# A key search's closing mask from tie count and stored signs, with the first heads' norm factors made by ScalarE and GpSimd

## The chip, the cores and the metric

The kernel runs on one core of a Trainium2 chip, as one launch. The metric is the device time in microseconds (us), as the median of several executions. TensorE does the matrix products, VectorE, ScalarE and GpSimd work on tiles of 128 partitions, and SyncE starts the transfers. In rows of the profile they are PE (PEld for its weight loads), DVE, ACT, POOL and SP.

## The reference

The program is a streaming encoder of two layers over 1024 positions of width 1024. The first layer is a sparse attention: an indexer gives each query a score for every admissible key, the 256 best keys are kept, and a grouped-query attention (16 heads in 4 groups, head size 64) runs over them, with RMS-normalised queries and keys. A banded attention and two convolutional feed-forward blocks follow.

```python
def dsa_mixer(h, w_in, q_g, k_g, t5_table):
    proj = h @ w_in
    q, k, v, qi, ki, wi = jnp.split(proj, list(A_SPLITS), axis=-1)
    q = rmsnorm(q.reshape(B, S, KV_GROUPS, Q_PER_KV, HEAD_DIM), q_g)
    k = rmsnorm(k.reshape(B, S, KV_GROUPS, HEAD_DIM), k_g)
...
        score = jnp.where(admissible[None], score, -jnp.inf)
        sel_score, sel = lax.top_k(score, topk)
        valid = jnp.isfinite(sel_score)
        k_sel = jax.vmap(lambda kb, ib: kb[ib])(k, sel)
```

`rmsnorm` divides by the root of the mean square of the 64 numbers of a head, plus 1e-6. On ties `top_k` keeps the keys that come first.

## The kernel before

The program is a chain of stages, each a block with one hand-written order of instructions per engine. An engine waits only on semaphores within a block, and all engines meet between two blocks. The head stage makes the scores SC, a tile with 4224 columns: six query tiles of 128 rows (tiles 2 to 7) that see 384, 512, 640, 768, 896 and 1024 keys, one behind the other. The first two query tiles see at most 256 keys and need no search.

The search stage (`select_phase`) finds for each query the value TH between kept and dropped keys. VectorE first turns the scores into ordered integers (ORD), then does two times 16 rounds, one bit each, over the high and then the low half of these integers. In a round VectorE counts the keys below TH in three of the six spans and ScalarE, by the sum of signs, in the other three. Three operations on 128x6 numbers close a round on VectorE: INC (was the count small enough), TH (the new threshold) and LESS (the half step of the next round). In the same stage TensorE makes the projections of queries, keys and values: four weight groups of eight tiles, 24 matmuls of 128x384 each. The weights come in two buffers, one transfer per group; the third group's transfer starts when TensorE has done its eighth tile. Each group is split into a high part WH (a cast) and a low part WL (a difference) in two halves; TensorE waits for the low parts (`w_lo`). For the first group ScalarE makes the casts and for the others GpSimd does. ScalarE takes the projected tiles out of PSUM (`take`), one per round, and the last three behind its signs.

At the end of the search VectorE marks the keys equal to TH and counts them (EQ, CNT, six operations), ranks these ties with six scans (RANK), and ScalarE sums the signs of TH minus the keys (SGN) into a scrap tile. From CNT and SGN follows how many ties may stay (ROOM). Six DROP operations mark the ties of too high a rank, and six MASK operations join them with the keys below TH.

The attention stage (`dsa_phase`) works in passes over pairs of heads. In the first pass it also makes the first group's queries and keys: GpSimd squares a tile's five heads (`raw_square`), VectorE sums them (`variance`), GpSimd takes the power -0.5 (`root`) and multiplies into DUP (`scaled`), TensorE turns DUP into TQ, ScalarE and VectorE split it into high and low part, and the logits follow. GpSimd's order is square 0, square 1, root 0, DUP 0, the blanking of the bias tile BB, and then square, root and DUP of one tile after the other. The other three groups are made the same way during later passes.

## Time and profile before

| what | value |
|---|---|
| median of 3 runs | 3011.78 us (3011.35 to 3015.06) |
| profiled execution | 3010.81 us |
| its span, first to last instruction | 3008.6 us |
| granted TensorE clock, mean | 0.973 |
| TensorE matmuls | busy 2792.0 us (93%) |
| VectorE | 1525.4 us (51%) |
| ScalarE | 1111.2 us (37%) |
| GpSimd | 840.1 us (28%) |
| mean of GpSimd's 128x1024 low part (L291, 132 times) | 2523 ns |

The busy times overlap, so they say which engine has the most work and not which one sets the end of a stage. A granted clock of 1.0 is TensorE's full 2.4 GHz, 0.5 is 1.2 GHz. For a change that touches the seam of two stages, the instructions in order of time around the seam are the rows to read.

### The profile page before, as it was taken

How to read it: one execution, taken by the hardware profiler on the slowest of the kernel's cores; microseconds unless marked ns; L12 is line 12 of the kernel's file. 1: busy time of each engine (PE TensorE's matmuls, PEld its weight loads, DVE VectorE, ACT ScalarE, POOL GpSimd, SP SyncE). 2: the span in 40 equal slices, each digit the busy share in tenths (PEclk: the TensorE clock that was granted, in tenths of full speed). 3: DMA queues.
4: the chain of work that ended last, by engine and by line, in shares of the span. 5: the costliest groups of instructions: out<-in, count | busy, mean ns of one | idle time of the engine just before them, and what ended most of it. 6: DMA issues, size and time to landing. Idle time of an engine off the chain costs nothing. (4 is left out here: it accounts for less than half of the span.)

```text
span 3008.6 us, 38734 instructions
## 1 busy us (share of the span) xinstructions
PE 2792.0 (93%) x14678; PEld 2388.8 (79%) x14678; DVE 1525.4 (51%) x2431; ACT 1111.2 (37%) x2392; POOL 840.1 (28%) x479
## 2 busy tenths in 40 slices
PE   6797698999999999999989986888999999999999
PEld 5697587887788888888879986777877888888887
DVE  5899665651544444544441113777515444444444
ACT  4677465551322222222245534666413222222221
POOL 4021523202332232232244431111023223232221
PEclk9899799999999999999989998999999999999999
DMA  4110000011211111111031100001012111111111
GB/s 162 42 43 1 25 5 8 14 52 42 71 49 49 42 43 54 42 50 50 12 130 43 43 21 1 12 26 68 8 36 77 50 42 52 45 42 56 49 42 63
DMA packets 38754, 132.43 MB, mean 44 GB/s; under 512 B 4240, under 2 KB 12608, under 8 KB 36960
## 3 DMA queue, kind: packets, MB, share of 16 engines
q1 hardware_dynamic: 38624, 130.68, 13.0%
q8 instruction: 83, 1.36, 0.2%
q14 instruction: 47, 0.39, 0.0%
HBM read 122.22 MB, written 13.69 MB: 45 GB/s over the span
## 5 line engine op out<-in xcount | busy, mean ns | idle before, releaser
L330 PE MATMUL banks<-XH,WH 128*128 128x512 f32 x1408 | 446.1, 397 | 5.3 <-POOL WL L291 4.2
L330 PE MATMUL banks<-XL,WH 128*128 128x512 f32 x1408 | 444.2, 396 | 0.0
L330 PE MATMUL banks<-XH,WL 128*128 128x512 f32 x1408 | 444.1, 396 | 0.0
L291 POOL TENSOR_TENSOR WL<-WR,WH 128x1024 fp32r<-128x1024 f32 x132 | 332.1, 2523 | 389.4 <-ACT WH L245 389.4
L260 ACT ACTIVATE Y<-U,CONVB,CONVW 128x1024 f32<-128x1024 f32 x88 | 109.5, 1244 | 659.7 <-DVE U L386 659.7
L386 DVE TENSOR_TENSOR U<-banks,RB 128x1024 f32<-128x1024 f32 x88 | 107.8, 1225 | 433.8 <-PE banks L330 424.5
L330 PEld LDWEIGHTS banks<-XH,WH 128*128 128x128 f32 x1408 | 265.4, 189 | 70.4 <-POOL WL L291 4.4
L330 PEld LDWEIGHTS banks<-XL,WH 128*128 128x128 f32 x1408 | 265.6, 189 | 64.2
L330 PEld LDWEIGHTS banks<-XH,WL 128*128 128x128 f32 x1408 | 265.3, 188 | 64.2
L376 DVE TENSOR_TENSOR XT<-XT,banks 128x1024 f32<-128x1024 f32 x176 | 214.6, 1219 | 164.7 <-PE banks L346 164.7
L299 POOL TENSOR_TENSOR AL<-Y,AH 128x1024 fp32r<-128x1024 f32 x44 | 106.0, 2410 | 625.5 <-ACT AH L268 625.5
L346 PE MATMUL banks<-AH,WH 128*128 128x512 f32 x704 | 219.4, 393 | 0.2 <-DVE XT L376 0.2
L346 PE MATMUL banks<-AL,WH 128*128 128x512 f32 x704 | 217.0, 389 | 0.0
L346 PE MATMUL banks<-AH,WL 128*128 128x512 f32 x704 | 216.8, 389 | 0.0
L245 ACT ACTIVATE WH<-WR 128x1024 fp32r<-128x1024 f32 x132 | 136.2, 1046 | 195.8 <-PE banks L346 101.7
L394 DVE SCALAR_TENSOR_TENSOR Y<-U,CONVW,Y 128x1022 f32<-128x1022 f32 x88 | 197.5, 2244 | 8.8 <-DVE Y L388 0.9
L771 PE MATMUL banks<-QWH,XH 128*128 128x384 f32 x512 | 179.1, 350 | 8.5 <-POOL QWL L717 8.5
L388 DVE SCALAR_TENSOR_TENSOR Y<-U,CONVW,Y 128x1023 f32<-128x1023 f32 x88 | 113.0, 1284 | 138.1 <-ACT Y L260 138.1
L771 PE MATMUL banks<-QWL,XH 128*128 128x384 f32 x512 | 177.6, 347 | 0.0
L771 PE MATMUL banks<-QWH,XL 128*128 128x384 f32 x512 | 176.7, 345 | 0.0
L346 PEld LDWEIGHTS banks<-AH,WH 128*128 128x128 f32 x704 | 130.6, 188 | 32.4 <-DVE XT L376 6.1
L346 PEld LDWEIGHTS banks<-AL,WH 128*128 128x128 f32 x704 | 132.2, 188 | 28.0
(225 smaller groups left out, 5462.9 us busy)
## 6 DMA issues: line engine op xcount, KB each, us to landing
WR<-in_ffn SPq DMA_DIRECT2D x132, 512.0 KB, 3.4
QWR<-in_qkv SPq DMA_DIRECT2D x12, 1536.0 KB, 6.7
XT<-in_xT SPq DMA_DIRECT2D x16, 512.0 KB, 7.8
OWR<-in_w_o SPq DMA_DIRECT2D x16, 512.0 KB, 3.2
spill<-XT SPq DMA_DIRECT2D x8, 512.0 KB, 14.6
XT<-spill SPq DMA_DIRECT2D x8, 512.0 KB, 7.1
outT<-XT SPq DMA_DIRECT2D x8, 512.0 KB, 2.6
near<-strip SPq DMA_DIRECT2D x1, 3072.0 KB, 21.3
```

Of the source, the lines that this page charges most:

```text
L245: act.activation(WH[:, ch % RING, :], WR[:, ch % RING, :], ACT.Copy).then_inc(w_hi, 1)
L260: act.activation(Y[:, j, k, :], U[:, k, :], ACT.Identity, bias=c.CONVB[:, layer, bass.ds(tap, 1)], scale=c.CONVW[:, layer, 2, bass.ds(tap, ...
L291: pool.tensor_tensor(WL[:, ch % RING, :], WR[:, ch % RING, :], WH[:, ch % RING, :].bitcast(F32), ALU.subtract).then_inc(w_lo, 1)
L299: pool.tensor_tensor(AL[:, g % 2, j, :], Y[:, j, 0, :], AH[:, g % 2, j, :].bitcast(F32), ALU.subtract).then_inc(a_lo, 1)
L330: mm = pe.matmul(u[:, h * HALF:(h + 1) * HALF], w[:, ch % RING, db * P:(db + 1) * P], x[:, db, h * HALF:(h + 1) * HALF], start=(db == 0 an ...
L346: mm = pe.matmul(DN[db % 2][:, h * HALF:(h + 1) * HALF], w[:, (ch + j) % RING, db * P:(db + 1) * P], x[:, g % 2, j, h * HALF:(h + 1) * HAL ...
L376: dve.tensor_tensor(c.XT[:, db, :], c.XT[:, db, :], DN[db % 2][:], ALU.add).then_inc(dn_free, 1)
L386: dve.tensor_tensor(U[:, k, :], UP[k][:], RB[:], ALU.mult).then_inc(scaled, 1)
L388: dve.scalar_tensor_tensor(Y[:, j, k, 1:S], U[:, k, 0:S - 1], c.CONVW[:, layer, 1, bass.ds(tap, 1)], Y[:, j, k, 1:S], ALU.mult, ALU.add).t ...
L394: dve.scalar_tensor_tensor(Y[:, j, k, 2:S], U[:, k, 0:S - 2], c.CONVW[:, layer, 0, bass.ds(tap, 1)], Y[:, j, k, 2:S], ALU.mult, ALU.add).t ...
L771: mm = pe.matmul(PJ[t % len(PJ)][:, 0:PROJ], x[:, db, i * P:(i + 1) * P], w[k % 2][:, db, :], start=(db == 0 and x is c.XH and w is WH), s ...
```

## The change

The signs of ScalarE are stored: SIDE holds, for each key, the sign of key minus TH (-1, 0 or 1), with the negated threshold NTH as bias. One operation per span then makes the mask: (RANK > ROOM) > SIDE is true for every key below TH (the left side is 0 or 1, and both are above -1), for a tie of too high a rank (1 > 0), and never for a key above TH. DROP and its six operations are gone, and so are ScalarE's waits between its signs. NTH is one operation more on VectorE, before the tie counts.

The mean squares of the first group's eight tiles are made in the search stage: after its last takes ScalarE runs 40 squares (8 tiles by 5 heads), each with its sum, and GpSimd makes variance and power -0.5 of all 40 numbers at once, into ROOTS. In the attention stage the first group's squares, variances and roots are gone, GpSimd starts with DUP 0 and DUP 1, and BB is blanked behind them. The casts of the first weight group move from ScalarE to GpSimd.

```diff
@@ -1163,24 +1164,26 @@
 
             def raw_square(t):
                 raw = c.qkv(t)[:, 0:NH * HD]
-                if t >= 2:
-                    pool.wait_ge(summed, t - 1)
+                if t >= TT + 2:
+                    pool.wait_ge(summed, t - TT - 1)
                 pool.tensor_tensor(SQ[:, t % 2, :], raw, raw, ALU.mult).then_inc(squared, 1)
 
             def root(t):
-                pool.wait_ge(var_ready, t + 1)
+                pool.wait_ge(var_ready, t - TT + 1)
                 pool.tensor_tensor(RS[:, t % TT, 0:NH], VAR[:, t % 2, 0:NH], c.NHALF[:, 0:NH],
                                    ALU.pow).then_inc(rs_ready, 1)
 
             def scaled(t):
-                pool.wait_ge(rs_ready, t + 1)
+                root_of = ROOTS[:, t, :] if t < TT else RS[:, t % TT, 0:NH]
+                if t >= TT:
+                    pool.wait_ge(rs_ready, t - TT + 1)
                 if t >= 2:
                     pool.wait_ge(turned, round_of_tile(t - 2) + 1)
                 pool.tensor_tensor(
                     DUP[:, t % 2, :].rearrange("p (h k d) -> p h k d", h=NH, k=2),
                     c.qkv(t)[:, 0:NH * HD].rearrange("p (h d) -> p h d", h=NH).unsqueeze(2)
                     .to_broadcast([P, NH, 2, HD]),
-                    RS[:, t % TT, 0:NH].unsqueeze(2).unsqueeze(3).to_broadcast([P, NH, 2, HD]),
+                    root_of.unsqueeze(2).unsqueeze(3).to_broadcast([P, NH, 2, HD]),
                     ALU.mult).then_inc(dup_ready, 1)
 
             def output_weights(db):
...
@@ -1188,15 +1191,11 @@
                 pool.tensor_tensor(OL[:, db % 2, :], OR[:, db % 2, :], OH[:, db % 2, :].bitcast(F32),
                                    ALU.subtract).then_inc(o_lo, 1)
 
-            raw_square(0)
-            raw_square(1)
-            for t in range(TT):
-                root(t)
+            scaled(0)
+            scaled(1)
+            pool.memset(BB[:, :, :, 0:S - W], 0.0).then_inc(b_blank, 1)
+            for t in range(2, TT):
                 scaled(t)
-                if t == 0:
-                    pool.memset(BB[:, :, :, 0:S - W], 0.0).then_inc(b_blank, 1)
-                if t + 2 < TT:
-                    raw_square(t + 2)
             for k in range(1, GROUPS):
                 for i in range(TT + 1):
                     if i < TT:
...
@@ -1320,12 +1319,12 @@
         @block.vector
         def _(dve):
             def variance(t):
-                dve.wait_ge(squared, t + 1)
-                if t >= 2:
-                    dve.wait_ge(rs_ready, t - 1)
+                dve.wait_ge(squared, t - TT + 1)
+                if t >= TT + 2:
+                    dve.wait_ge(rs_ready, t - TT - 1)
                 dve.tensor_reduce(SSQ[:, t % 2, 0:NH], SQ[:, t % 2, :].rearrange("p (h d) -> p h d", h=NH), AX.X,
                                   ALU.add).then_inc(summed, 1)
-                dve.wait_ge(summed, t + 1)
+                dve.wait_ge(summed, t - TT + 1)
                 dve.tensor_scalar(VAR[:, t % 2, 0:NH], SSQ[:, t % 2, 0:NH], 1.0 / HD, EPS, ALU.mult,
                                   ALU.add).then_inc(var_ready, 1)
 
...
@@ -1376,18 +1375,14 @@
                                   OP[:, 0:PAIR].rearrange("p (h d) -> p h d", h=2),
                                   RCP[:].unsqueeze(2).to_broadcast([P, 2, HD]), ALU.mult).then_inc(mo_ready, 1)
 
-            variance(0)
-            variance(1)
             queries_low(0, 0)
             others_low(0, None, 1)
-            variance(2)
             dve.wait_ge(b_blank, 1)
             mask(0)
             row_max(0)
             row_max(1)
             queries_low(1, 2)
             others_low(1, None, 3)
-            variance(3)
             row_max(2)
             queries_low(2, 4)
             others_low(2, None, 5)
...
@@ -1397,8 +1392,6 @@
                 if i >= 4:
                     dve.wait_ge(t_first, g + 1)
                     dve.tensor_copy(PT[:, g % 2, 0:HALF], TP[0][:]).then_inc(pt_dve, 1)
-                if p == 0 and h == 0 and i + EARLY + 1 < TT:
-                    variance(i + EARLY + 1)
                 if g + AHEAD < ALL:
                     row_max(g + AHEAD)
                 if has_round(g):
...
@@ -1848,13 +1841,16 @@
     with ExitStack() as ctx:
         sem, old = c.signals.open(ctx, f"s")
         QT = TT - FIRST_TOP
+        NH = DSA.nh
         m = Map(nc, c.after_scores, c.before_qkv)
         MASK, SC = c.MASK, c.SC
         ORD = nc.alloc_sbuf_tensor_at("ORD", [P, SC_ALL], I32, offset=c.scores_at)
         RANK = nc.alloc_sbuf_tensor_at("RANK", [P, SC_ALL], F32, offset=c.scores_at)
         REST = m.take("REST", [P, SC_ALL], F32)
         LOW = nc.alloc_sbuf_tensor_at("LOW", [P, SC_ALL], U16, offset=m.at)
-        DROP = m.take("DROP", [P, SC_ALL], BF16)
+        SIDE = m.take("SIDE", [P, SC_ALL], BF16)
+        SSQ = m.take("SSQ0", [P, TT, NH], F32)
+        VAR = m.take("QVAR0", [P, TT, NH], F32)
         EQ = MASK
         JUNKA = m.take("JUNKA", [P, 3, S], BF16)
         WH = m.take("QWH", [P, 2, DB, PROJ], F32R)
...
@@ -1906,12 +1904,15 @@
             pool.sem_clear(old)
             for k in range(GROUPS):
                 for h in range(2):
-                    if k >= 1:
-                        pool.wait_ge(w_landed[k % 2], 16 * (k // 2 + 1))
-                        pool.tensor_copy(WH[:, k % 2, half(h), :], WR[:, k % 2, half(h), :]).then_inc(w_hi, 1)
+                    pool.wait_ge(w_landed[k % 2], 16 * (k // 2 + 1))
+                    pool.tensor_copy(WH[:, k % 2, half(h), :], WR[:, k % 2, half(h), :]).then_inc(w_hi, 1)
                     pool.wait_ge(w_hi, 2 * k + h + 1)
                     pool.tensor_tensor(WL[:, k % 2, half(h), :], WR[:, k % 2, half(h), :],
                                        WH[:, k % 2, half(h), :].bitcast(F32), ALU.subtract).then_inc(w_lo, 1)
+            pool.wait_ge(squared, TT)
+            pool.tensor_scalar(VAR[:], SSQ[:], 1.0 / HD, EPS, ALU.mult, ALU.add).then_inc(var_ready, 1)
+            pool.wait_ge(var_ready, 1)
+            pool.tensor_tensor(c.ROOTS[:], VAR[:].rearrange("p t h -> p (t h)"), c.NHALF[:], ALU.pow)
 
         @block.tensor
         def _(pe):
...
@@ -1946,9 +1947,6 @@
                     if src is LOW and BETWEEN.stop + j < TILES - 3:
                         take(BETWEEN.stop + j)
 
-            act.wait_ge(w_landed[0], 16)
-            for h in range(2):
-                act.activation(WH[:, 0, half(h), :], WR[:, 0, half(h), :], ACT.Copy).then_inc(w_hi, 1)
             act.wait_ge(done, 2)
             count_signs(halves[:, :, 1], HIGH_STEP)
             act.wait_ge(done, K_REST + 1)
...
@@ -1958,13 +1956,19 @@
             for t in BETWEEN:
                 take(t)
             count_signs(LOW, LOW_STEP)
-            act.wait_ge(stepped, LOW_STEP + BITS)
+            act.wait_ge(done, K_END + 1)
             for q, off, n in spans:
-                act.activation(JUNKA[:, 0, 0:n], REST[:, off:off + n], ACT.Sign, bias=TH[:, q:q + 1], scale=-1.0,
+                act.activation(SIDE[:, off:off + n], REST[:, off:off + n], ACT.Sign, bias=NTH[:, q:q + 1],
                                accum_out=SGN[:, q:q + 1]).then_inc(signed, 1)
-                act.wait_ge(signed, spans.index((q, off, n)) + 1)
             for t in range(TILES - 3, TILES):
                 take(t)
+            junk = JUNKA[:].rearrange("p a n -> p (a n)")
+            for t in range(TT):
+                for h in range(NH):
+                    mm = act.activation(junk[:, (t * NH + h) * HD:(t * NH + h + 1) * HD],
+                                        c.qkv(t)[:, h * HD:(h + 1) * HD], ACT.Square,
+                                        accum_out=SSQ[:, t, h:h + 1])
+                mm.then_inc(squared, 1)
 
         @block.vector
         def _(dve):
...
@@ -2006,27 +2010,24 @@
             dve.wait_ge(done, K_END)
             find(LOW, LOW_STEP, BITS)
             dve.wait_ge(stepped, LOW_STEP + BITS)
+            dve.tensor_scalar(NTH[:], TH[:], -1.0, None, ALU.mult).then_inc(done, 1)
             for q, off, n in spans:
                 dve.tensor_scalar(EQ[:, off:off + n], REST[:, off:off + n], TH[:, q:q + 1], None, ALU.is_equal,
                                   ALU.add, accum_out=CNT[:, q:q + 1]).then_inc(done, 1)
             for q, off, n in spans:
                 eq = EQ[:, off:off + n]
-                dve.wait_ge(done, K_END + q + 1)
+                dve.wait_ge(done, K_END + q + 2)
                 dve.tensor_tensor_scan(RANK[:, off:off + n], eq, eq, 0.0, ALU.add, ALU.max).then_inc(done, 1)
 
-            k = K_END + 2 * QT
+            k = K_END + 1 + 2 * QT
             dve.wait_ge(signed, QT)
-            dve.tensor_tensor(INC[:], CNT[:], SGN[:], ALU.add).then_inc(done, 1)
+            dve.tensor_tensor(INC[:], CNT[:], SGN[:], ALU.subtract).then_inc(done, 1)
             dve.wait_ge(done, k + 1)
             dve.scalar_tensor_tensor(ROOM[:], INC[:], 0.5, CONST[:], ALU.mult, ALU.add).then_inc(done, 1)
             dve.wait_ge(done, k + 2)
             for q, off, n in spans:
-                dve.scalar_tensor_tensor(DROP[:, off:off + n], RANK[:, off:off + n], ROOM[:, q:q + 1],
-                                         EQ[:, off:off + n], ALU.is_gt, ALU.mult).then_inc(done, 1)
-            for q, off, n in spans:
-                dve.wait_ge(done, k + 3 + q)
-                dve.scalar_tensor_tensor(MASK[:, off:off + n], REST[:, off:off + n], TH[:, q:q + 1],
-                                         DROP[:, off:off + n], ALU.is_lt, ALU.add).then_inc(done, 1)
+                dve.scalar_tensor_tensor(MASK[:, off:off + n], RANK[:, off:off + n], ROOM[:, q:q + 1],
+                                         SIDE[:, off:off + n], ALU.is_gt, ALU.is_gt).then_inc(done, 1)
 
 
 class Chip:
...
@@ -2053,7 +2054,8 @@
         c.MH, c.ML = c.XH, c.XL
         c.IDF = m.take("IDF", [P, P], F32)
         c.ONES = m.take("ONES", [P, P], F32)
-        c.NHALF = m.take("NHALF", [P, TT], F32)
+        c.NHALF = m.take("NHALF", [P, TT * DSA.nh], F32)
+        c.ROOTS = m.take("ROOTS", [P, TT * DSA.nh], F32)
         c.RSTD = m.take("RSTD", [P, TT], F32)
         c.GAIN = m.take("GAIN", [P, 4, DB], F32)
         c.HGAIN = m.take("HGAIN", [P, 4], F32)
...
```

Not shown are declarations: new tiles for NTH, the name ROOTS in the attention stage, and the two semaphores `squared` and `var_ready` in the search stage.

## Rows read from the trace of the kernel before

**Rows 1.** Stretch, its length, busy us of PE, PEld, DVE, ACT, POOL; clock, DMA, GB/s.

```profile
284.30:310.10 25.80, 0.58 (x4) 0.26 (x2) 25.06 (x32) 7.37 (x15) 0.00 (x0) 0.59 0.00 0
```

**Rows 2.** VectorE in order of time (start us, us, engine, line, operation).

```profile
284.32 0.75 DVE L2010 TENSOR_SCALAR_CACHE_REDUCE MASK<-REST,TH 128x512 bf16<-128x512 f32 x1
...
299.01 5.26 DVE L2024 SCALAR_TENSOR_TENSOR DROP<-RANK,ROOM,MASK 128x512 bf16<-128x512 f32 x6
...
304.19 5.26 DVE L2028 SCALAR_TENSOR_TENSOR MASK<-REST,TH,DROP 128x512 bf16<-128x512 f32 x6
```

**Rows 3.** GpSimd in order of time, opening of the attention stage.

```profile
310.11 1.40 POOL L1168 TENSOR_TENSOR SQ<-QKVA 128x320 f32<-128x320 f32 x2 [76.37 <-POOLq L1848]
...
312.88 1.26 POOL L1179 TENSOR_TENSOR DUP<-QKVA,RS 128x640 f32<-128x640 f32 x1
314.08 2.66 POOL L1197 MEMSET BB<- 128x3072 f32 x1
```

**Rows 4.** ScalarE in order of time, end of the search.

```profile
281.54 0.82 ACT L1942 ACTIVATE JUNKA<-LOW,TH 128x640 bf16<-128x640 uint16 x1
...
282.36 1.13 ACT L1942 ACTIVATE JUNKA<-LOW,TH 128x1024 bf16<-128x1024 uint16 x1
...
290.36 1.52 ACT L1935 ACTIVATE QKVB<-banks,RSTD 128x384 f32<-128x384 f32 x3
```

**Rows 5.** ScalarE in order of time, the later stage's squares.

```profile
1562.45 0.31 ACT L641 ACTIVATE JUNK<-banks,RSTD 128x64 bf16<-128x64 f32 x1
...
1562.74 0.31 ACT L641 ACTIVATE JUNK<-banks,RSTD 128x64 bf16<-128x64 f32 x1
```

**Rows 6.** GpSimd's roots, one line of each place (ns min/median/max).

```profile
L1172 POOL TENSOR_TENSOR RS<-QVAR,NHALF x32: 1167/1167/1169, 311.6 to 550.4; 128x5 f32<-128x5 f32 x32
...
L1658 POOL TENSOR_TENSOR RSTD<-VAR,NHALF x1: 1652/1652/1652, 47.7 to 47.7; 128x8 f32<-128x8 f32 x1
...
L157 POOL TENSOR_TENSOR RSTD<-VAR,NHALF x3: 2619/2619/2621, 775.4 to 2266.2; 128x8 f32<-128x8 f32 x3
```

**Rows 7.** ScalarE in order of time, start of the search.

```profile
142.02 2.86 ACT L1951 ACTIVATE QWH<-QWR 128x1536 fp32r<-128x1536 f32 x2 [8.73 <-DMA QWR<-in_qkv]
```

**Rows 8.** GpSimd in order of time, weights of the projections.

```profile
143.58 6.88 POOL L1913 TENSOR_TENSOR QWL<-QWR,QWH 128x1536 fp32r<-128x1536 f32 x2 [75.19 <-ACT QWH L1951]
150.40 1.46 POOL L1911 CAST QWH<-QWR 128x1536 fp32r<-128x1536 f32 x1
151.94 3.50 POOL L1913 TENSOR_TENSOR QWL<-QWR,QWH 128x1536 fp32r<-128x1536 f32 x1
...
190.20 1.47 POOL L1911 CAST QWH<-QWR 128x1536 fp32r<-128x1536 f32 x1 [29.75 <-DMA QWR<-in_qkv]
```

**Rows 9.** TensorE in order of time, projections and the attention's second turn.

```profile
147.07 0.69 PE L1926 MATMUL banks<-QWH,XH 128*128 128x384 f32 x1 [15.12 <-POOL QWL L1913]
...
152.04 0.49 PE L1926 MATMUL banks<-QWH,XH 128*128 128x384 f32 x1
...
284.55 0.34 PE L1926 MATMUL banks<-QWH,XL 128*128 128x384 f32 x1
...
319.93 1.11 PE L1224 MATMUL banks<-IDF,DUP 128*128 128x128 f32 x4 [0.61 <-POOL DUP L1179]
```

**Rows 10.** VectorE in order of time, in the search.

```profile
138.20 4.56 DVE L1989 TENSOR_TENSOR ORD<-SC,REST 128x4224 int32<-128x4224 int32 x1
...
147.52 2.95 DVE L1980 TENSOR_TENSOR INC<-CNT,KEEP 128x6 f32<-128x6 f32 x1 [1.53 <-ACT JUNKA L1942]
...
151.91 3.56 DVE L1974 TENSOR_SCALAR LESS<-TH,BITF 128x6 f32<-128x6 f32 x1
...
158.16 2.31 DVE L1980 TENSOR_TENSOR INC<-CNT,KEEP 128x6 f32<-128x6 f32 x1
...
190.77 0.92 DVE L1980 TENSOR_TENSOR INC<-CNT,KEEP 128x6 f32<-128x6 f32 x1
```

**Rows 11.** GpSimd in order of time, first feed-forward stage.

```profile
778.03 7.66 POOL L291 TENSOR_TENSOR WL<-WR,WH 128x1024 fp32r<-128x1024 f32 x2
```

More of the change, by code:

```diff
@@ L1016, in dsa_phase @@
         RS = m.take("RS0", [P, TT, 8], F32)
+        ROOTS = c.ROOTS[:].rearrange("p (t h) -> p t h", h=NH)
         NM = m.take("NM0", [P, 8], F32)
@@ L1865, in select_phase @@
         LESS = m.take("LESS", [P, QT], F32)
+        NTH = m.take("NTH", [P, QT], F32)
         INC = m.take("INC", [P, QT], F32)
@@ L1874, in select_phase @@
         counted, off_done, signed = sem("counted"), sem("off_done"), sem("signed")
+        squared, var_ready = sem("squared"), sem("var_ready")
         w_landed = [sem("w_even"), sem("w_odd")]
```

## The prediction

> **What bounds the kernel now.** I read the page first. TensorE is busy for 93% of the span (the table above), but that is a mean over stages, and the change sits in the one long hole: the table of stretches shows TensorE with 0.58 us of work in the 25.8 us from 284.3 to 310.1, VectorE with 25.06 and the granted clock down at 0.59 [rows 1]. There the engines' order of time decides, so I read the timeline of each engine. VectorE works without a gap: tie marks and counts from 284.32, six scans, six DROP operations (5.26), six MASK operations (5.26), ended at 309.45 [rows 2]. Then the next stage opens: GpSimd's first instruction at 310.11, 0.66 us after VectorE's end, and two squares, a root and the first DUP follow; the DUP, which TensorE waits for, starts at 312.88 [rows 3]. So the path is: end of the search, VectorE to 309.45, 0.66 of stage change, 2.77 of GpSimd work, DUP. ScalarE has nothing to do after about 291.9 [rows 4]. That free time is what the change fills, and the question is whether the filling ends before VectorE does.
>
> **VectorE's part.** DROP goes: minus 5.26. The new MASK operation has DROP's operands (an f32 tile, a column, a bf16 tile), so it costs 5.26, as DROP did. One small NTH operation comes in: LESS, its like, has its successor 0.14 us after it, so plus 0.14. VectorE would end at 304.3 (309.45 - 5.26 + 0.14).
>
> **ScalarE's part.** The signs start after NTH, at 284.31 + 0.22 = 284.53 (0.17 to run and 0.05 to signal; an estimate). Without the waits between them they run as the search's own counts do: 640 elements take 0.82 from start to start; for 1024 the sum starts 1.04 and the next operation would start 1.13 after the start (as long as the record is) [rows 4]. That is 0.30 + 0.81 per 1000 elements, and six signs over 4224 elements give 1.8 + 3.4 = 5.2: ended at 289.7. The three takes need 1.5 [rows 4]: 291.2. Then forty squares of 64 elements, each with a sum. The nearest row is the later stage's squares, one per 0.29 us from start to start, reading PSUM [rows 5]: 11.6 us. By the line just fitted for SBUF sources, 64 elements take 0.30 + 0.05 = 0.35: 14.0. The new squares read SBUF, so I take nearly that, 0.335 (13.4). The squares end at 304.6; the bounds are 302.8 and 305.2.
>
> **GpSimd's part.** The variance of 40 elements has no row; the bounds are 0.1 (nothing but a signal) and 0.8, and I take 0.3 plus 0.2 of signals. The root is a power of 128x40. Rows: 1.167 us for 5 elements, 1.652 for 8, and another stage's 2.62 for 8 [rows 6]. The first two give 0.162 per element and 0.36 fixed; 40 elements are then 6.8 us. With 2.62 the slope is 0.282 and the root 11.6. The 5-element roots work on the very numbers that the new root works on and never differ by more than 2 ns, so I take 6.8. GpSimd ends at 304.6 + 0.5 + 6.8 = 311.9, later than VectorE's 304.3 and later than the old end, 309.45. The stage change, again 0.66, leads to 312.6, where DUP is now the first instruction: before it was 312.88. The 5.26 taken from VectorE and the 2.77 taken from the opening come to 8.0, and the new chain on ScalarE and GpSimd gives back 7.7: **minus 0.3** (from -2.8 with the cheap squares and variance to +5.6 with dear squares, variance and root).
>
> **The opening of the attention.** The second DUP no longer waits for a root: TensorE's 0.61 of idle time ahead of its turn at 319.93 goes [rows 9], and the turns behind it, each of which waits for the one before, pass that on. The eight variances leave VectorE too, at a place where it mostly waits for the others; I give them 0.1 of gain. The blanking of BB (2.66) now stands behind two DUPs of 1.26 [rows 3], from 2.5 to 5.2 us after the first DUP's start. Its reader needs the first logits as well, and these stand just ahead of TensorE's turn at 319.93, some 6 us after that start [rows 3, 9], so the blanking costs nothing; with a faster first turn it would cost what it sticks out. Sum: **minus 0.7** (0 to -1.7).
>
> **The other end: the first weight group.** ScalarE made the high part of group 0 in 2.86 us from 142.02 [rows 7]; now GpSimd does, in front of each of its two low parts. GpSimd's pace is 4.99 us per half: 1.54 from a cast's start to its low part's, and 3.45 for the low part (two took 6.88) [rows 8]. These are the dangerous rows, because VectorE's smallest operations stand still behind GpSimd's: INC, normally 0.17, took 2.95 and ended with GpSimd's low part at 150.5; LESS took 3.56, just as long as the low part from 151.94 [rows 8, 10]. The counts themselves run beside it: from that LESS's end at 155.45 to the next INC at 158.16 they take 2.7, with a cast and a low part running [rows 10]. The reverse happens too: two of GpSimd's operations of a kind that takes 2.5 on average (the table above) took 7.66 beside VectorE's [rows 11]. So GpSimd's first cast, whose weights are there at 142.02, should wait for VectorE's ORD, which ends at 142.76 [rows 10].
>
> The Trainium skill (SBUF — State Buffer, "SBUF: two separate sides") calls the pair of ports that the two engines share an exclusive lock, held for the whole instruction, also by a VectorE operation with two SBUF inputs when GpSimd reads SBUF. By it the cast starts at 142.8; without it at 142.0, and the sum of this part would be 0.5 instead of 1.3. The trace agrees with the rule at every small operation named above.
>
> Step by step, with halves at 142.80, 147.79, 152.78 and 157.77, GpSimd is done at 162.8 (before 160.45). LESS waits for the cast (144.3), counts to 147.0, INC waits to 147.8, TH to 149.3, LESS to 152.8, counts to 155.5, INC to 157.8, TH to 159.3, LESS to 162.8, counts to 165.5, TH done 166.0. Before, the INC of 158.16 ended at 160.5 and its TH 0.3 later, and the third TH, one undisturbed round of 3.4 on, at 164.1 [rows 10]: the search is 1.9 late here. TensorE: its first low part is ready at 147.75 (0.7 late); twelve matmuls at 0.33 (147.07 to 152.04 are fifteen steps) [rows 9] bring it to 151.7, and the second low part comes at 152.75, a wait of 1.1. Before, sixteen had started by 152.04, and the rest went at 0.176 (752 in 132.5 us) [rows 9]. Its thirteenth now starts at 152.8, six or seven full-speed steps behind, and a first matmul is 0.17 longer: 1.3 late. If the pause keeps the clock at 0.5 for some ten matmuls more, add 1.5: 2.8.
>
> Group 2's weights start after TensorE's eighth tile, so GpSimd's conversion of 190.20 [rows 8] moves by TensorE's 1.3, to 191.5, and its cast ends at 193.0. INC, issued at 190.77 [rows 10], comes 1.9 later, at 192.6, still inside the cast. So it is released in the same place as before, TH and LESS too, and the search leaves group 2 late by exactly GpSimd's shift, 1.3; group 3 keeps the same distance. TensorE's own 1.3 are covered: ScalarE takes the last tiles at 290.36, 5.5 us after the last matmul began [rows 4, 9]. **Plus 1.3** for the rest of the kernel (0.5 to 2.8; 4.0 with the rival below).
>
> **Sum.** -0.3 - 0.7 + 1.3 = +0.3 us. The profiled execution took 3010.81 for a span of 3008.6 (2.2 lie around it) and is 1.0 under the median of 3011.78. So 3011.1 for a like execution, 3012.1 as a median. This kernel's measurement can tell 0.2% (6 us) from no change.
>
> **Rivals.** (1) *VectorE sets the end*, since squares and root are cheaper than their rows: DUP starts at 304.3 + 0.66 = 305.0 instead of 312.88; -7.9 - 0.7 + 1.3 = -7.3, 3004.5. For it speaks only the change's arithmetic; against it the 0.29 per square even at the lower bound, which puts ScalarE's end at 302.8 and leaves 1.5 us for variance and root. Chance 0.05. (2) *The root is dear*, on the other side: GpSimd's 40-element power at 0.282 per element costs 11.6, +4.8: +5.1, 3016.9. It is slower by over 0.2% from 0.31 per element on. The other stage's row speaks for it, the 32 equal 5-element rows against. Chance 0.11. (3) *The search loses a slot*: if TensorE is under 1.0 late, or the search over 2.2, INC at group 2 meets the 3.5 us low part instead of the cast; counts that had run beside the second low part then run behind it, +2.7: +3.0, 3014.8. My margin is 0.35 us. Chance 0.15. (4) *The moved cast costs nothing in the search* and the squares go by the lower bound: -0.3 - 1.8 - 0.7 = -2.8, 3009.0. Chance 0.10. The forecast itself: 0.59, with its own range of 3010 to 3014.
>
> **How the numbers follow.** The range takes in (3) and (4) and most of (2): 3008.5 to 3017. Faster by over 0.2% needs (1): 0.06, with a little for what I do not see. Slower by over 0.2% needs (2) with (3) or with the dear bounds of other terms: 0.09. Within 0.2%: 0.85.
>
> **What would show it.** The last MASK operation near 305.6 (304.3 + 1.3), the squares ending near 305.9, the 128x40 power lasting 6.8 and ending near 313, the first DUP 0.7 us after it, at 313.9 against 312.88. In the search: the first INC ending at 147.8, the third TH at 166.0, the group 2 cast at 191.5, the first tie count at 285.8 instead of 284.32. Wrong would be a power far from 6.8, squares far from 0.335 apart, or a search end that is not TensorE's shift.

## The result, and the profile after

The changed kernel takes **2988.0 us** (2985.2 to 2991.5) against 3013.4 (3011.4 to 3015.6) for the kernel before on the same chip: ratio 0.9916, with an interval of 0.9899 to 0.9933. It is 25 us faster, where 3012.1 was forecast and 3008.5 was the bottom of the range. The profiled execution has a span of 2985.7 (before 3008.6), and the mean granted clock is 0.972 against 0.973, so the clock is not the answer.

First the place where the change was made. The kernel after, VectorE, ScalarE, GpSimd and TensorE at the end of the search, in order of time on each engine (start us, us, engine, line, operation):

```profile
303.01 5.28 DVE L2029 SCALAR_TENSOR_TENSOR MASK<-RANK,ROOM,SIDE 128x512 bf16<-128x512 f32 x6
...
293.65 1.49 ACT L1936 ACTIVATE QKVB<-banks,RSTD 128x384 f32<-128x384 f32 x3
295.04 0.25 ACT L1968 ACTIVATE JUNKA<-QKVA 128x64 bf16<-128x64 f32 x1
...
295.28 0.25 ACT L1968 ACTIVATE JUNKA<-QKVA 128x64 bf16<-128x64 f32 x1
...
304.77 1.07 POOL L1913 TENSOR_SCALAR QVAR<-SSQ 128x40 f32<-128x40 f32 x1 [67.12 <-ACT JUNKA L1968]
305.93 6.98 POOL L1915 TENSOR_TENSOR ROOTS<-QVAR,NHALF 128x40 f32<-128x40 f32 x1
313.57 2.47 POOL L1182 TENSOR_TENSOR DUP<-QKVA,ROOTS 128x640 f32<-128x640 f32 x2 [0.67 <-POOLq L1841]
...
314.88 1.11 PE L1223 MATMUL banks<-IDF,DUP 128*128 128x128 f32 x4 [27.74 <-POOL DUP L1182]
```

The first DUP starts at 313.57; before it started at 312.88 [rows 3], and 313.9 was forecast. So the seam is 0.7 us later than before, and nothing was won there. The first matmul of each stage says where the 22.9 us of span went. TensorE's rows of the kernel before, in order of time:

```profile
314.19 1.12 PE L1224 MATMUL banks<-IDF,DUP 128*128 128x128 f32 x4 [29.31 <-POOL DUP L1179]
...
672.72 0.48 PE L1285 MATMUL banks<-XH,OWH 128*128 128x512 f32 x1
...
1529.37 0.69 PE L771 MATMUL banks<-QWH,XH 128*128 128x384 f32 x1 [8.31 <-POOL QWL L717]
...
2163.41 0.48 PE L848 MATMUL banks<-XH,OWH 128*128 128x512 f32 x1
```

and of the kernel after (its first matmul of the attention, 314.88, is shown above):

```profile
674.91 0.48 PE L1284 MATMUL banks<-XH,OWH 128*128 128x512 f32 x1
...
1522.09 0.69 PE L771 MATMUL banks<-QWH,XH 128*128 128x384 f32 x1 [8.71 <-POOL QWL L717]
...
2151.80 0.48 PE L848 MATMUL banks<-XH,OWH 128*128 128x512 f32 x1
```

| stage | before | after | difference |
|---|---|---|---|
| up to the attention's first matmul | 314.19 | 314.88 | +0.7 |
| attention | 358.53 | 360.03 | +1.5 |
| output projection and feed-forward | 856.65 | 847.18 | -9.5 |
| second projections and attention | 634.04 | 629.71 | -4.3 |
| output projection and feed-forward | 845.19 | 833.90 | -11.3 |

All of the gain lies in stages whose code the change doesn't touch, and there it is spread evenly. One place in the second feed-forward, TensorE in order of time, shows it. Before:

```profile
2399.68 0.63 PE L330 MATMUL banks<-XL,WH 128*128 128x512 f32 x2
2400.15 0.63 PE L330 MATMUL banks<-XH,WL 128*128 128x512 f32 x2
2400.62 0.63 PE L330 MATMUL banks<-XH,WH 128*128 128x512 f32 x2
```

After:

```profile
2399.61 0.62 PE L330 MATMUL banks<-XH,WH 128*128 128x512 f32 x2
2400.06 0.62 PE L330 MATMUL banks<-XL,WH 128*128 128x512 f32 x2
2400.52 0.62 PE L330 MATMUL banks<-XH,WL 128*128 128x512 f32 x2
```

There is no bracket with idle time in either; the clock is full. Two matmuls take 0.47 from start to start before and 0.455 after. Over hundreds of steps (572 and 573 between 1000 and 1200 us, those of over 300 ns left out) the pace is **233.3 ns before and 229.0 after** for 128x512 (L330), and 176.0 against 173.3 for 128x384 (L771, over 1,000 each). The down-projections (L346) stay at 227.1 and 227.5. There are 4,224 matmuls of L330, 768 of the two output projections (232.4 to 228.9) and 1,536 of L771: 4,224 x 4.35 ns is 18.4, 768 x 3.5 is 2.7 and 1,536 x 2.67 is 4.1, together 25.2 us, and the last three rows of the table give 25.1. The kernels' instructions are the same there; what differs is the SBUF address of their tiles. The change widened NHALF from 8 to 40 numbers and added ROOTS, another 40, ahead of nearly everything in the memory map: the tiles of these stages lie 320 bytes higher. XH and XL, allocated ahead of NHALF, stay.

### The profile page after: what moved, and what is told of

Its sections match the earlier page's. It is cut to its first block and busy times, and to the rows that moved or that the text cites. A ratio compares the mean times of both kernels' runs of the same rounds, so it can differ in the third digit from the quotient of the medians.

```text
span 2985.7 us, 38732 instructions
## 1 busy us (share of the span) xinstructions
PE 2768.3 (93%) x14646; PEld 2387.3 (80%) x14678; DVE 1518.5 (51%) x2410; ACT 1117.7 (37%) x2470; POOL 837.7 (28%) x467
## 5 line engine op out<-in xcount | busy, mean ns | idle before, releaser
L330 PE MATMUL banks<-XH,WH 128*128 128x512 f32 x1408 | 439.8, 394 | 5.0 <-POOL WL L291 4.2
L330 PE MATMUL banks<-XL,WH 128*128 128x512 f32 x1408 | 440.5, 394 | 0.0
L330 PE MATMUL banks<-XH,WL 128*128 128x512 f32 x1408 | 436.4, 391 | 0.0
L330 PEld LDWEIGHTS banks<-XH,WH 128*128 128x128 f32 x1408 | 265.5, 189 | 62.8 <-POOL WL L291 4.3
L330 PEld LDWEIGHTS banks<-XH,WL 128*128 128x128 f32 x1408 | 265.3, 188 | 61.0
L330 PEld LDWEIGHTS banks<-XL,WH 128*128 128x128 f32 x1408 | 265.6, 189 | 58.0
L346 PE MATMUL banks<-AH,WH 128*128 128x512 f32 x704 | 218.8, 392 | 0.0
L346 PE MATMUL banks<-AL,WH 128*128 128x512 f32 x704 | 217.4, 390 | 0.0
L346 PE MATMUL banks<-AH,WL 128*128 128x512 f32 x704 | 216.8, 389 | 0.0
L771 PE MATMUL banks<-QWH,XH 128*128 128x384 f32 x512 | 177.8, 347 | 8.9 <-POOL QWL L717 8.9
L771 PE MATMUL banks<-QWL,XH 128*128 128x384 f32 x512 | 176.3, 344 | 0.0
L771 PE MATMUL banks<-QWH,XL 128*128 128x384 f32 x512 | 175.4, 343 | 0.0
L346 PEld LDWEIGHTS banks<-AH,WH 128*128 128x128 f32 x704 | 130.6, 188 | 30.6 <-DVE XT L376 4.5
L346 PEld LDWEIGHTS banks<-AH,WL 128*128 128x128 f32 x704 | 132.1, 188 | 28.2
```

What stands on the lines that cost most here:

```text
L330: mm = pe.matmul(u[:, h * HALF:(h + 1) * HALF], w[:, ch % RING, db * P:(db + 1) * P], x[:, db, h * HALF:(h + 1) * HALF], start=(db == 0 an ...
L346: mm = pe.matmul(DN[db % 2][:, h * HALF:(h + 1) * HALF], w[:, (ch + j) % RING, db * P:(db + 1) * P], x[:, g % 2, j, h * HALF:(h + 1) * HAL ...
L771: mm = pe.matmul(PJ[t % len(PJ)][:, 0:PROJ], x[:, db, i * P:(i + 1) * P], w[k % 2][:, db, :], start=(db == 0 and x is c.XH and w is WH), s ...
```

## The experiments

Two theories were open after that. *Placement*: TensorE's pace hangs on the addresses; padding alone gives the gain and the change at the old addresses gives none of it. *The change's own work*: freeing VectorE and GpSimd at the seam speeds something up later. A matmul's row names two operands: the one with 128*128 is called stationary here, the one with 512 or 384 columns moving. Below, "distance" is the address of the moving tile minus that of the stationary one in L330, modulo 256 bytes: XH lies at 33,920 and WH of the feed-forward at 119,040, so it is 128 before and 64 after (XL and WL lie at the same places modulo 256). The expectations of pad320_again and pad192 count it the other way round, so that their 192 is 64 here and their 64 is 192.

**pad320.** The kernel before, with an unused tile of 320 bytes behind NHALF:

```
 c.NHALF = m.take("NHALF", [P, TT], F32)
+m.take("PAD", [P, 80], F32)
```

> The kernel before with one unused tile of 320 bytes per partition behind NHALF, so that every tile behind it lies 320 bytes higher, as in the changed kernel; no instruction changes. Theory A, placement: the pace of the matmuls follows where the stationary and the moving operand lie in SBUF. Then the up-projections (L330) go at 0.229 us from start to start instead of 0.233 and the band projections at 0.173 instead of 0.176, and the kernel takes 2988 to 2991. Theory B, the change's own instructions gave the time: the pace stays at 0.233 and the time at 3013.

Measured: 2994.6 (2993.5 to 2997.6), ratio 0.9931 [0.9918, 0.9945]; L330 at 229.0. Twenty of the 25 us come from a tile that nobody reads; the 2988 to 2991 of the expectation was missed by 4. In this profile L771 ran at 176.7; the very same kernel, profiled once more, is below.

**after_old.** The whole change, with every tile of before at its old address: NHALF 8 wide, the 40-wide constant and ROOTS in a gap behind other tiles, SSQ, VAR and NTH behind the old tiles of the select stage.

```
-c.NHALF = m.take("NHALF", [P, TT * DSA.nh], F32)
-c.ROOTS = m.take("ROOTS", [P, TT * DSA.nh], F32)
+c.NHALF = m.take("NHALF", [P, TT], F32)
+c.XHALF = nc.alloc_sbuf_tensor_at("XHALF", [P, TT * DSA.nh], F32, offset=c.before_qkv - 384)
+c.ROOTS = nc.alloc_sbuf_tensor_at("ROOTS", [P, TT * DSA.nh], F32, offset=c.before_qkv - 192)
```

> The changed kernel with all tiles that the kernel before has at their old addresses (the new tiles ROOTS, SSQ, VAR, NTH and a 40-element exponent tile lie in room that was free). Theory A: the matmul paces are those of before, 0.233 and 0.176, and only the seam is left: 3011 to 3014, within 0.2% of before. Theory B: 2988 as the changed kernel.

Measured: 3012.2 (3006.2 to 3013.9), ratio 0.9989 [0.9980, 0.9998]; L330 at 233.3. This is the edit as the prediction had priced it. GpSimd and TensorE in order of time:

```profile
303.48 6.98 POOL L1916 TENSOR_TENSOR ROOTS<-QVAR,XHALF 128x40 f32<-128x40 f32 x1
311.13 2.47 POOL L1182 TENSOR_TENSOR DUP<-QKVA,ROOTS 128x640 f32<-128x640 f32 x2 [0.67 <-POOLq L1842]
...
312.44 1.12 PE L1223 MATMUL banks<-IDF,DUP 128*128 128x128 f32 x4 [26.04 <-POOL DUP L1182]
```

**The mask alone and the casts alone.** mask_old has only SIDE, NTH and the one mask operation (norm factors and casts as before, old addresses); after_old_casts is after_old with the first group's casts back on ScalarE.

```
(in short)
-ACT.Sign, bias=TH[:, q:q + 1], scale=-1.0        (into JUNKA)
+ACT.Sign, bias=NTH[:, q:q + 1]                   (into SIDE)
-DROP = (RANK > ROOM) * EQ ;  MASK = (REST < TH) + DROP
+MASK = (RANK > ROOM) > SIDE
```

> The kernel before with the first half of the change alone: the signs stored in SIDE and one mask operation per span; norm factors as before, the first weight group's casts on ScalarE, all old tiles at their old addresses. My theory of the seam: VectorE ends 5.1 us earlier, nothing else moves, so the time falls by 5.1 us (ratio 0.9983) and the paces are those of before. Rival: the second half carries part of the gain, and this half alone gives under 3 us.

> The changed kernel with all old tiles at their old addresses and the first weight group's two casts back on ScalarE. My theory: the search loses nothing any more, so it is 1.3 to 1.5 us faster than the same kernel with the casts on GpSimd, and about 4 us faster than before (ratio 0.9986). Rival: the casts cost nothing where they are, and the time is that of the kernel with casts on GpSimd (0.9989).

Measured: mask_old 3009.6 (3005.4 to 3011.7), ratio 0.9983 [0.9974, 0.9992]; after_old_casts 3009.3 (3007.6 to 3011.8), ratio 0.9982 [0.9973, 0.9991]. mask_old, GpSimd and TensorE:

```profile
306.11 1.39 POOL L1168 TENSOR_TENSOR SQ<-QKVA 128x320 f32<-128x320 f32 x2 [71.27 <-POOLq L1848]
...
308.88 1.26 POOL L1179 TENSOR_TENSOR DUP<-QKVA,RS 128x640 f32<-128x640 f32 x1
...
310.19 1.11 PE L1224 MATMUL banks<-IDF,DUP 128*128 128x128 f32 x4 [24.60 <-POOL DUP L1179]
```

The mask alone starts the attention at 310.19, earlier than the whole change (312.44). The early norm factors add 1.6 to it (311.75 in after_old_casts), and the moved casts another 0.7. The three intervals overlap, so the times don't tell these kernels apart, nor whether the casts cost the 1.3 to 1.5 us of the expectation; the order is that of the profiles.

**Which addresses.** More or less padding, and the whole map moved by 128 bytes with XH and XL in it, so that no distance changes:

```
+m.take("PAD", [P, 16], F32)      (pad64; 32, 48, 64 numbers for pad128, pad192, pad256)

-m = Map(nc, (nc.sbuf_base + 63) // 64 * 64, top - 2 * 4 * S)
+m = Map(nc, (nc.sbuf_base + 63) // 64 * 64 + 128, top - 2 * 4 * S)      (base128)
```

> The kernel before with 64 bytes more in front of the later tiles. Theory A with a period of 256 bytes in the distance between the two operands: weights then lie at 64 modulo 256 and XH at 128, as after the change, so L330 goes at 0.229 and the kernel takes about 2990. If the size of the shift matters in another way (period 1024 or more), the pace can stay at 0.233.

> The kernel before with 128 bytes more in front of the later tiles: weights and XH then have the same address modulo 256, as weights and AH of the down-projections have already (0.228). Theory A with a period of 256 in the distance: L330 at 0.228 to 0.229. If what counts is that the weights' address is no multiple of 128, L330 stays at 0.233.

> The kernel before with all of its SBUF map 128 bytes higher, XT, XH and XL too, so that the distances between weights and XH stay as they were and only the absolute addresses change. If the distance of the two operands sets the pace, L330 stays at 0.233 and the projections at 0.176; if the absolute address of one of them does (weights at 128 modulo 256, as with the 128 bytes of padding behind XH), L330 goes at 0.227.

> The kernel before with 256 bytes more in front of the tiles behind NHALF. If the pace repeats every 256 bytes of distance, L330 is back at 0.233 and the time at about 3013; if only the old place was bad, it is 0.227 to 0.229.

> 192 bytes of padding, the last of the four places modulo 256: the weights' distance to XH is then 64 modulo 256. If the pace depends on how far the distance is from 128, L330 goes at 0.229, as with 64 and 320 bytes (distance 192); time about 2994. A pace of 0.227 or 0.233 would say that the dependence is not symmetric.

> The very kernel with 320 bytes of padding once more. Its band projections went at 0.1767, though all tiles of that stage lie where the changed kernel has them, which went at 0.1733. If such a pace changes from execution to execution, it may now read 0.1733; if the program fixes it, 0.1767 again. L330 at 0.229 in either case.

| kernel | distance | L330 | L771 | L346 | out. proj. to end | time |
|---|---|---|---|---|---|---|
| before | 128 | 233.3 | 176.0 | 227.1 | 2335.9 | 3010.8 |
| after_old | 128 | 233.3 | 176.0 | 226.9 | 2333.5 | 3012.2 (median) |
| base128 | 128 | 233.3 | 176.0 | 227.1 | 2335.8 | 3014.5 |
| pad256 | 128 | 233.3 | 176.0 | 227.1 | 2335.7 | 3011.2 |
| pad64 | 64 | 229.0 | 173.3 | 227.4 | 2312.8 | 2996.1 |
| pad320 | 64 | 229.0 | 176.7 | 227.6 | 2317.2 | 2994.6 (median) |
| pad320_again | 64 | 229.0 | 173.3 | 227.3 | 2311.0 | 2994.5 |
| after | 64 | 229.0 | 173.3 | 227.5 | 2310.8 | 2988.0 (median) |
| pad128 | 0 | 226.7 | 173.3 | 227.2 | 2301.9 | 2983.9 |
| pad192 | 192 | 233.3 | 173.3 | 227.1 | 2332.8 | 3011.3 |

(Paces in ns from start to start, steps of over 300 ns left out, L330 and L346 from 1000 to 1200 us and L771 from 1580 to 1760; the last column but one from the first output projection's start to the end of the span; times in us, where not a median, of the profiled execution. In L771 the weights move and XH is stationary, so there 64 and 192 change places.) The pace goes by the distance and not by either address alone: the weights stand 128 bytes higher in pad128 and in base128 alike, and only the one where XH stays is fast. The down-projections move with their own input AH, keep their distance of 0, and their pace, whether both operands stand 0, 64, 128 or 192 bytes behind a multiple of 256: most of their steps are 226 or 227 ns, as in the up-projections of pad128. (The expectation's 0.228 for them has a few pauses of over 300 ns in its mean.) Distances of 64 and 192 were each run with one pair of addresses modulo 256 only. Each of the two extreme cases in the second feed-forward, TensorE in order of time. pad128:

```profile
2399.59 0.62 PE L330 MATMUL banks<-XH,WH 128*128 128x512 f32 x2
2400.04 0.62 PE L330 MATMUL banks<-XL,WH 128*128 128x512 f32 x2
2400.49 0.61 PE L330 MATMUL banks<-XH,WL 128*128 128x512 f32 x2
```

base128:

```profile
2399.81 0.63 PE L330 MATMUL banks<-XH,WL 128*128 128x512 f32 x2
2400.28 0.63 PE L330 MATMUL banks<-XH,WH 128*128 128x512 f32 x2
```

pad192 was the miss: with a distance of 192 I had counted on the pace of 64, as if only how far apart the two are mattered. L330 read 233.3 instead. So it matters which of the two is ahead, or 64 and 192 differ for a reason that these runs don't show. The equal means of 128 and 192 hide different steps: at 128 they alternate between 229 or 230 ns and 237 or 238, the long one between the two matmuls that share a stationary tile, and at 192 nearly all are 233 or 234; at 64 they go round 226, 229 and 232. For 384 columns only distance 128 is slow. The pad320 profile's 176.7 at L771 does not come from the placement alone: the same kernel read 173.3 the second time, so one profile's pace at L771 is weaker evidence than L330's, which followed the distance in all 14 profiles.

The times of single executions hold more than the pace. In the profiles of pad64, pad128 and pad320_again the search loses some 4 us near 225 us (told below), and their attention begins at 318.5 to 319.4, where pad320, base128, pad256 and pad192 read 313.6 to 314.8. That is a part of why pad64 missed its 2990.

**The best placement, timed.** pad128 again, and mask_pad128: the mask half of the change with 128 bytes of padding.

> The kernel before with 128 bytes of padding again, now timed. From the paces of its first look (L330 at 0.2267 for 4224 matmuls, 0.0066 less than before: 28 us; band projections 1536 by 0.0027: 4 us; output projections 768 by 0.0055: 4 us; projections of the search stage are behind the search, and the head stage loses about 1): 35 us less than before, 2979 to 2985. Rival: part of that was one lucky execution, and the timed gain is under 26 us.

> The better version from both findings: the first half of the change alone (signs stored, one mask operation), casts on ScalarE, and 128 bytes of padding. If the two gains add, it is 5 us under the kernel with the padding alone, at 2975 to 2980, and faster than the changed kernel (2988) by 8 us or more. Rival: with TensorE at the faster pace the seam no longer counts, and it is level with the padding alone.

Measured: pad128_timed 2979.6 (2978.2 to 2980.2), ratio 0.9885 [0.9869, 0.9902]; mask_pad128 **2972.9** (2972.5 to 2973.5), ratio 0.9865 [0.9848, 0.9881], the fastest kernel of this study, 15 us under the change as made. The padding's gain came as expected. With the mask the time is 6.7 under the padding alone, where 5 was expected, and below the stated 2975 to 2980; the rival (level with the padding alone) is out.

## Why the prediction was wrong

**The step that failed** is one that the prediction took without saying: "**Plus 1.3** for the rest of the kernel", where the rest was carried over unmoved, matmul for matmul. The prediction went through the diff operation by operation, and passed over two lines of it, the allocation of NHALF and ROOTS, as if memory cost nothing. Their effect was -25 us (from 672.72 and 674.91 on, the last three rows of the table of stages), more than three times the largest gain that any rival allowed for. pad320 gets it without the change, after_old loses it with the change.

The Trainium skill (SBUF — State Buffer, "SBUF: two separate sides") says that TensorE never waits on anyone at SBUF's engine ports. No run here tests it against another engine; what they show is that the distance of TensorE's own two operands moves its pace, from 226.7 to 233.3 ns with the same instructions on every engine.

**The edit itself**, at the old addresses, was forecast at +0.3 us and measured at -0.11% of 3012, or -3 us, with an interval from -0.6 to -6; in the profiles the attention begins 1.75 earlier (312.44 against 314.19). That is below the 0.2% that the measurement can tell, and just at the lower edge of the range (0.9989 x 3011.8 = 3008.5). Term by term:

- *Mask in one operation*: right. The six take 5.28, and 5.26 are gone. mask_old starts the attention 4.0 earlier although its tie count starts later; its ratio makes 5 us of it.
- *Squares*: mis-sized. They came every 0.24 us, not 0.335, under even my lower bound of 0.29 [rows 5]. Those squares read PSUM and are scaled by a column of RSTD (`scale=c.RSTD`), while the new ones read SBUF and have no such scale; which of the two makes the difference was not tested. 40 of them: 9.6 instead of 13.4.
- *Variance*: 1.07 for 128x40 on GpSimd where 0.3 was taken, and 1.16 with the signal.
- *Root*: 6.98, taken as 6.8. The 11.6 of the dear root [rows 6] did not come. Rival (2) is out, and so is (1): ScalarE, GpSimd's variance and root still set the end, 5.3 us behind the last MASK (308.29 against 313.57).
- *The low end of this sum*: -2.8 was an error of adding. 302.8 + 0.1 + 6.8 + 0.66 is 310.4, 2.5 under 312.88.
- *The moved casts*: the mechanism was right in after_old, to within 0.5: the first INC ends at 148.1, the third TH starts at 166.0, the third group's conversion at 192.0, where 147.8, 166.0 and 191.5 were said, and TensorE paused 0.74 ahead of 153.09, with a select stage that began 0.5 late. The tie count came 1.0 late beyond that, so the moved cast was not free, as rival (4) had it. GpSimd's first cast did wait for ORD, which ends at 143.92 in the kernel after: its record is 1.91 long instead of 1.46 and ends at 145.25. In the kernel after, the search was 2.8 late rather than 1.3, as much as the prediction's dear case, but not by its steps. The third group's cast started at 194.53, 3.2 late once the stage's own late start is taken off, and INC met the 3.5 us low part there (196.85, below), as rival (3) had it. The search had done one more round before it than in the kernel before, so it did not lose rival (3)'s whole 2.7.

The kernel after, search, in order of time, GpSimd, then VectorE, then TensorE:

```profile
143.34 1.91 POOL L1908 CAST QWH<-QWR 128x1536 fp32r<-128x1536 f32 x1 [73.58 <-DMA QWR<-in_qkv]
...
194.53 1.47 POOL L1908 CAST QWH<-QWR 128x1536 fp32r<-128x1536 f32 x1 [30.87 <-DMA QWR<-in_qkv]
196.08 3.51 POOL L1910 TENSOR_TENSOR QWL<-QWR,QWH 128x1536 fp32r<-128x1536 f32 x1
...
150.22 3.51 DVE L1978 TENSOR_SCALAR LESS<-TH,BITF 128x6 f32<-128x6 f32 x1
...
156.42 2.25 DVE L1984 TENSOR_TENSOR INC<-CNT,KEEP 128x6 f32<-128x6 f32 x1
...
160.12 3.56 DVE L1978 TENSOR_SCALAR LESS<-TH,BITF 128x6 f32<-128x6 f32 x1
...
196.85 2.76 DVE L1984 TENSOR_TENSOR INC<-CNT,KEEP 128x6 f32<-128x6 f32 x1
...
148.81 0.69 PE L1927 MATMUL banks<-QWH,XH 128*128 128x384 f32 x1 [15.69 <-POOL QWL L1910]
...
153.75 0.69 PE L1927 MATMUL banks<-QWH,XH 128*128 128x384 f32 x1 [0.73 <-POOL QWL L1910]
```

The matmul behind the pause took 0.69 and the clock was still halved: fourteen matmuls, the last of them at 158.07, started some 0.32 us apart, where the prediction's dear case had ten. The granted clock of two stretches of four us says the same (stretch, length, busy us of PE, PEld, DVE, ACT and POOL, clock, DMA share, GB/s). Before:

```profile
152.00:156.00 4.00, 4.00 (x23) 4.00 (x23) 4.00 (x2) 2.57 (x6) 4.00 (x2) 0.95 0.01 2
156.00:160.00 4.00, 4.00 (x25) 4.00 (x24) 3.96 (x7) 0.00 (x0) 3.92 (x2) 1.00 0.01 2
```

After:

```profile
152.00:156.00 4.00, 3.27 (x11) 2.76 (x10) 4.00 (x6) 0.87 (x2) 3.92 (x3) 0.50 0.02 4
156.00:160.00 4.00, 4.00 (x19) 4.00 (x18) 3.93 (x4) 0.00 (x0) 4.00 (x2) 0.71 0.01 2
```

The clock that stayed low and the 1.2 us by which the select stage began late (ORD at 139.36 against 138.20 [rows 10]) put ScalarE's signs 2.6 later than forecast (they wait for NTH and start at 288.45, where 284.53 + 1.3 = 285.8 follows from the prediction; VectorE's tie count starts at 288.32); cheap squares give 3.8 back, variance and root take 0.9: 313.9 + 2.6 - 3.8 + 0.9 = 313.6, and 313.57 was measured. The forecast of the seam was nearly right because two errors cancelled.

**A slot like rival (3)'s** was lost elsewhere too. Two profiles of the kernel with 128 bytes of padding reach the attention's first matmul at 319.35 and at 314.10; 1.1 of the 5.25 is there already as the first projection starts. Near 225 us GpSimd converts the last weight group. GpSimd and VectorE, in the one profile (pad128),

```profile
225.57 3.62 POOL L1913 TENSOR_TENSOR QWL<-QWR,QWH 128x1536 fp32r<-128x1536 f32 x1
...
224.08 1.76 DVE L2004 TENSOR_SCALAR LOW<-REST 128x640 uint16<-128x640 f32 x1
225.76 4.52 DVE L2002 TENSOR_TENSOR REST<-REST,ORD 128x1024 f32<-128x1024 f32 x1
...
232.29 3.27 DVE L1974 TENSOR_SCALAR LESS<-TH,BITF 128x6 f32<-128x6 f32 x1
```

and VectorE in the other (pad128_timed)

```profile
221.41 0.49 DVE L2004 TENSOR_SCALAR LOW<-REST 128x640 uint16<-128x640 f32 x1
221.81 1.22 DVE L2002 TENSOR_TENSOR REST<-REST,ORD 128x1024 f32<-128x1024 f32 x1
...
230.14 3.55 DVE L1974 TENSOR_SCALAR LESS<-TH,BITF 128x6 f32<-128x6 f32 x1
```

The same operation takes 4.52 behind GpSimd's difference of 225.57 and 1.22 ahead of any. It took 4.5 in the profiles of pad64 and pad320_again as well, and 1.22 in the other eleven. What decides it is not shown: the search starts 1.3 us later in pad128 than in pad128_timed, but pad192 and pad64 start only 0.1 apart (138.97 and 139.08), and only pad64 loses the slot. Such a slot, some 4 us, is as large as the whole edit at the old addresses.

**Not settled.** Why 64 and 192 differ; why L771 read 176.7 in one profile of pad320 and 173.3 in the next; why the select stage starts up to 2.3 us later in some profiles; and the 1.7 to 2.4 us that after_old and mask_old gain behind the attention. No theory of the chip's inside was tested for the distance, only that the pace goes with it. Tiles of other engines moved against XH too; that it is TensorE's own pair is inferred from the down-projections, whose pair kept its distance and whose pace stayed.

## What to carry to other kernels

Read the allocations in a diff like its instructions: a new tile of a few bytes ahead of the matmul operands moves them, and here that was worth eight times the edit. Before crediting an edit with a gain, look whether untouched stages changed their pace, and time the edit once at the old addresses and once the addresses without the edit. A kernel bound by TensorE is worth a sweep of padding in steps of 64 bytes before any rescheduling: 128 bytes gave 34 us here, with matmuls of 512 and 384 columns of 4-byte numbers; other types were not run.

## What the runs showed of the hardware

- **Operand distance.** 128x512 matmuls start every 226.7, 229.0, 233.3 and 233.3 ns at a distance of 0, 64, 128 and 192 bytes modulo 256; 128x384 every 173.3 at 0, 64 and 192 and 176.0 at 128 (one profile of pad320 apart). At the best distance the 128 columns between the two cost 226.67 - 173.33 = 53.3 ns, 0.417 ns each, which is one cycle of the full clock, and 13.3 ns per matmul are left over in both.
- **The clock after a short pause.** In the attention TensorE waits 2.2 us for a DUP near 550 us. After it the clock is full in one profile and halved for some 7 us in another. The kernel before, and mask_old (same columns as above):

```profile
548.00:552.00 4.00, 2.66 (x25) 2.46 (x22) 2.24 (x8) 1.91 (x7) 1.59 (x2) 1.00 0.00 0
552.00:556.00 4.00, 3.15 (x26) 2.88 (x27) 1.22 (x3) 1.30 (x4) 2.01 (x2) 1.00 0.00 0
```

```profile
548.00:552.00 4.00, 2.30 (x12) 2.30 (x12) 0.53 (x3) 0.77 (x2) 2.86 (x3) 0.64 0.00 0
552.00:556.00 4.00, 4.00 (x19) 3.60 (x20) 1.32 (x5) 0.97 (x5) 0.10 (x1) 0.50 0.00 0
556.00:560.00 4.00, 3.97 (x17) 2.93 (x15) 2.03 (x8) 2.87 (x9) 1.15 (x1) 0.58 0.00 0
```

  The pause is as long in both, 2.19 and 2.18. mask_old loses 3.3 us there, and with it most of the 4.0 that it had won at the seam: its attention takes 362.7 against 358.5. Nothing shows this to be the mask's doing: base128, which has the instructions of the kernel before, takes 362.1. Over all 14 profiles the attention takes 358.5 in the two with a granted clock of 1.00 from 540 to 575 us (before and pad256), 358.5 to 361.6 in those with 0.95 or 0.90 but for pad320_again (362.1), and 362.0 to 362.7 in the four with 0.85. The kernel after (0.90, 360.0) is among them, so the +1.5 us of its attention in the table of stages need not be the edit's.
- **ScalarE's short sums.** A 64-element square with its sum comes every 0.24 us from SBUF without a scale column, and every 0.29 from PSUM with one [rows 5].
- **GpSimd.** The power of 40 elements takes 6.98 and a two-operation scale of the same 40 takes 1.07.
